# Sample attentions: values of the first four sequences weighed between the key chunks of the other four, loads queued in that order, three key banks

## The reference, cut to what matters

```python
# B: dilated windows over a cache of 2048 keys, 4 heads x 64, 8 sequences
logit = einsum('nthe,ntjhe->nthj', q, kg) + bias        # per dilation group (128,1), (512,4), (2048,16)
out   = merge_by_denominators(stats)                    # softmax over the union, multiplicities by the groups
# C: sparse attention over 4096 cached keys, 256 of them selected per query by an indexer
logit = einsum('nqhe,nqkhe->nqhk', q, kg) + bias        # only selected keys
out   = einsum('nqhk,nqkhe->nqhe', softmax(logit), vg)
```

## Time and profile before

| what | us |
|---|---|
| timed runs, median of 3 | 3127.01 (3124.59 to 3127.49) |
| profiled execution | 3129.59 |
| its span | 3127.8 |
| stage B (1449.2 to 1589.7) | 140.5 |
| stage C (1589.7 to 1834.8) | 245.1 |
| mlp (1834.8 to the end) | 1293.0 |

### The profile page before, as it was taken

The page is one execution under the profiler, slowest core; times in us unless marked ns, Lnnn a source line. Parts: engine busy times, 40 slices in busy tenths (PEclk is TensorE's granted clock), DMA queues, the critical chain, the costliest instruction groups (busy, mean ns, idle before and its releaser), DMA issues. The chain is left out here.

```text
span 3127.8 us, 33968 instructions
## 1 busy us (share of the span) xinstructions
PE 2659.0 (85%) x13588; PEld 1692.1 (54%) x13604; DVE 1136.5 (36%) x2070; ACT 666.8 (21%) x1346; POOL 366.8 (12%) x352
## 2 busy tenths in 40 slices
PE   7999995085788987886638769999999999999998
PEld 3444442032667776454425434566666666888843
DVE  0007999655666665484615202100000000000033
ACT  1122221032334544574303200100000000000011
POOL 1000000101444431000016520000000000000000
PEclk9999997576799999798768879999999999999999
DMA  6111110241335532414779772301101113110010
GB/s 238 51 42 51 41 41 20 100 114 39 112 97 161 150 126 77 155 38 131 254 216 359 284 269 101 115 27 40 40 27 40 40 28 105 39 38 29 11 34 33
DMA packets 170291, 305.86 MB, mean 98 GB/s; under 512 B 48536, under 2 KB 121448, under 8 KB 167866
## 3 DMA queue, kind: packets, MB, share of 16 engines
q1 hardware_dynamic: 145154, 175.87, 18.0%
q0 software_dynamic: 23136, 93.01, 8.2%
q10 hardware_dynamic: 1864, 35.08, 3.3%
HBM read 262.76 MB, written 68.29 MB: 106 GB/s over the span
## 5 line engine op out<-in xcount | busy, mean ns | idle before, releaser
L929 PE MATMUL m_B<-m_big,m_wdB 128*128 128x363 f32 (+1 forms) x2112 | 646.1, 468 | 3.2 <-issue 3.2
L929 PEld LDWEIGHTS m_B<-m_big,m_wdB 128*128 128x128 f32 x2112 | 400.4, 190 | 248.0 <-issue 5.0
L384 PE MATMUL i_psM<-i_w,i_xnT 128*128 128x477 f32 x1024 | 418.3, 567 | 2.3 <-ACT i_xnT L232 2.3
L384 PEld LDWEIGHTS i_psM<-i_w,i_xnT 128*128 128x128 f32 x1024 | 192.8, 191 | 213.5 <-issue 206.5
L791 DVE TENSOR_TENSOR m_actT<-m_wdB,m_B 128x363 f32 (+3 forms) x66 | 35.1, 532 | 604.1 <-PE m_B L929 604.1
L683 ACT ACTIVATE m_wdB<-m_B 128x363 f32<-128x363 f32 (+1 forms) x66 | 31.2, 473 | 599.0 <-PE m_B L929 599.0
L971 PE MATMUL m_B<-m_wdA,m_actT 128*128 128x256 f32 x704 | 152.4, 379 | 0.8 <-DVE m_actT L791 0.8
L971 PE MATMUL m_B<-m_wdB,m_actT 128*128 128x256 f32 x704 | 152.6, 379 | 0.0
L971 PEld LDWEIGHTS m_B<-m_wdA,m_actT 128*128 128x128 f32 x704 | 133.7, 190 | 19.5 <-DVE m_actT L791 1.4
L971 PEld LDWEIGHTS m_B<-m_wdB,m_actT 128*128 128x128 f32 x704 | 133.5, 190 | 18.8 <-issue 0.8
L649 POOL TENSOR_TENSOR m_rstd<-m_ms,m_half 128x1 f32<-128x1 f32 x18 | 9.9, 553 | 1133.3 <-DVE m_ms L759 1133.3
(11 more groups left out here) (414 smaller groups left out, 3587.0 us busy)
## 6 DMA issues: line engine op xcount, KB each, us to landing
b_Kp<-b_k SPq DMA_DIRECT2D x32, 512.0 KB, 10.5
b_Vp<-b_v SPq DMA_DIRECT2D x32, 512.0 KB, 11.2
o_bk<-b_k ACTq DMA_DIRECT2D x8, 2040.0 KB
o_bv<-b_v ACTq DMA_DIRECT2D x8, 2040.0 KB
i_w<-w_in POOLq DMA_DIRECT2D x8, 1908.0 KB, 29.9
proj<-i_stage SPq DMA_DIRECT2D x64, 238.5 KB, 2.0
m_wdB<-w_gate SPq DMA_DIRECT2D x22, 512.0 KB, 4.0
m_wdB<-w_up SPq DMA_DIRECT2D x22, 512.0 KB, 5.2
```

The lines of the kernel that those rows point to most:

```text
L384: mm = nc.tensor.matmul(psM[:, c % 2, 0:CHW], xnT[:, t % 2, k, :], w[:, k, c * CHW:(c + 1) * CHW], start=(k == 0), stop=(k == KO - 1))
L929: mm = nc.tensor.matmul(B[:, bank, 0:r1 - r0], wgu[:, i, u, k, :], hnT[:, k, r0:r1], start=(k == 0), stop=(k == KO - 1))
```

## The change

Transposed probabilities get a bank of their own (4) while keys are still transposed, and keys keep three (0, 1, 3). For the chunks behind the key loop, probabilities use all four. The first NCH - 1 chunks of the first group (MIXED: 3 in B, 7 in C) are transposed, copied and weighed inside the key loop, one in each step from chunk NCH + 1 on (LAG = 1): `turn_keys(ch+1)`, `turn_probs(k)`, `products(ch)`, `weigh(k)` with k = ch - NCH - 1. ACT's order follows: the copy of probabilities k stands behind the copies of the next chunk's keys, and the exponential of the second group behind the last copy of the first group. The load queue takes values between key chunks in the order in which they are wanted. DVE's order is unchanged but for the bank number.

```diff
...
     TOT = KEYS + DEC
     COL = COL_C if sparse else COL_B
     KS, VS = 8, 12
-    TURN_BANKS = (0, 1, 3, 4)
+    TURN_BANKS, PROB_BANK = (0, 1, 3), 4
+    LAG = 1
+    MIXED = NCH - LAG
+    prob_bank = lambda k: PROB_BANK if k < MIXED else (0, 1, 3, 4)[(k - MIXED) % 4]
     LOGIT_BANKS = (2, 7)
     with ExitStack() as ctx:
         sb = lambda n, s, dt=F32: ctx.enter_context(nc.sbuf_tensor(f"{tag}_" + n, s, dt))
...
                             eng.wait_ge(S["pv"], (k - VS) // 4 + 1)
                         piece_dma(eng, "c_v" if sparse else "b_v", k, Vp[:, k % VS, :], V_in[k % VS])
 
-                keys(range(2 * CH))
-                values(range(VS))
-                keys(range(2 * CH, 4 * CH))
-                values(range(VS, 4 * CH))
+                chunk = lambda ch: range(4 * ch, 4 * ch + 4)
+                ready = VS // 4
+                for ch in range(NCH):
+                    keys(chunk(ch))
+                    if ch >= NCH - ready:
+                        values(chunk(ch - NCH + ready))
+                for ch in range(NCH, CH):
+                    keys(chunk(ch))
+                    if ch - 2 >= NCH + LAG:
+                        values(chunk(ch - 2 - NCH - LAG + ready))
+                for ch in range(max(MIXED - 2, 0) + ready, CH):
+                    values(chunk(ch))
 
             @block.sync
             def _(sp):
...
                     act.wait_ge(S["keysT"], b + 1)
                     if ch >= 2:
                         act.wait_ge(S["products"], ch - 1)
-                    nc.scalar.activation(KpT[:, ch % 2, n, i, :], B[:, TURN_BANKS[b % 4], :], ACT.Copy)\
+                    nc.scalar.activation(KpT[:, ch % 2, n, i, :], B[:, TURN_BANKS[b % 3], :], ACT.Copy)\
                         .then_inc(keysT_out[i], 1)
 
                 def softmax(g):
...
                     nc.scalar.activation(logit[:, g, :], logit[:, g, :], ACT.Exp, bias=nmx[:, g:g + 1],
                                          accum_out=den[:, g:g + 1]).then_inc(S["prob"], 1)
 
+                def evac_probs(k):
+                    act.wait_ge(S["probT"], k + 1)
+                    if k >= 2:
+                        act.wait_ge(S["pv"], k - 1)
+                    nc.scalar.activation(PT[:, k % 2, :, :],
+                                         B[:, prob_bank(k), :].rearrange("p (j q) -> p j q", j=4),
+                                         ACT.Copy).then_inc(S["PT"], 1)
+
                 for ch in range(CH):
                     for n in range(4):
                         for i in range(1 if sparse else 2):
                             evac_keys(4 * ch + n, i)
-                    if ch == NCH + 1:
+                    if ch == NCH + LAG:
                         softmax(0)
+                    if ch > NCH + LAG:
+                        evac_probs(ch - 1 - NCH - LAG)
+                for k in range(MIXED - 1, NCH):
+                    evac_probs(k)
                 softmax(1)
-                for k in range(CH):
-                    act.wait_ge(S["probT"], k + 1)
-                    if k >= 2:
-                        act.wait_ge(S["pv"], k - 1)
-                    nc.scalar.activation(PT[:, k % 2, :, :],
-                                         B[:, TURN_BANKS[k % 4], :].rearrange("p (j q) -> p j q", j=4),
-                                         ACT.Copy).then_inc(S["PT"], 1)
+                for k in range(NCH, CH):
+                    evac_probs(k)
 
             @block.vector
             def _(dve):
...
                     dve.wait_ge(S["keysT"], b + 1)
                     if ch >= 2:
                         dve.wait_ge(S["products"], ch - 1)
-                    nc.vector.tensor_copy(KpT[:, ch % 2, n, i, :], B[:, TURN_BANKS[b % 4], :])\
+                    nc.vector.tensor_copy(KpT[:, ch % 2, n, i, :], B[:, TURN_BANKS[b % 3], :])\
                         .then_inc(keysT_out[i], 1)
 
                 def logits(g, c):
...
                         pe.wait_ge(K_in[k % KS], 16 * (k // KS + 1))
                         for i in range(2):
                             b = 2 * k + i
-                            if k >= 2:
-                                pe.wait_ge(keysT_out[i], k - 1)
+                            if b >= 3:
+                                pe.wait_ge(keysT_out[(b - 3) % 2], (b - 3) // 2 + 1)
                             for j in range(4):
-                                mm = tp(B[:, TURN_BANKS[b % 4], P * j:P * j + P],
+                                mm = tp(B[:, TURN_BANKS[b % 3], P * j:P * j + P],
                                         Kp[:, k % KS, B_W * j + P * i:B_W * j + P * i + P], ident[:, :])
                             mm.then_inc(S["keysT"], 1)
 
...
                 if sparse:
                     pe.wait_ge(spread_at, 1)
                     pe.wait_ge(unsel_in, 32)
-                for ch in range(CH):
-                    if ch + 1 < CH:
-                        turn_keys(ch + 1)
-                    products(ch)
-                    if ch % NCH == NCH - 1:
-                        new_products(ch // NCH)
 
                 def turn_probs(k):
                     g, c = k // NCH, k % NCH
-                    if k >= 4:
-                        pe.wait_ge(S["PT"], k - 3)
+                    before = max(k - 3, MIXED if k - MIXED >= 3 else 0) if k >= MIXED else k
+                    if before:
+                        pe.wait_ge(S["PT"], before)
                     if c == 0:
                         pe.wait_ge(S["prob"], g + 1)
                     for j in range(4):
-                        mm = tp(B[:, TURN_BANKS[k % 4], P * j:P * j + P], logit[:, g, 512 * c + P * j:512 * c + P * j + P],
+                        mm = tp(B[:, prob_bank(k), P * j:P * j + P], logit[:, g, 512 * c + P * j:512 * c + P * j + P],
                                 ident[:, :])
                     mm.then_inc(S["probT"], 1)
 
-                turn_probs(0)
-                for k in range(CH):
+                def weigh(k):
                     g, c = k // NCH, k % NCH
-                    if k + 1 < CH:
-                        turn_probs(k + 1)
                     if c == 0:
                         if g:
                             pe.wait_ge(S["out"], 1)
...
                         mm.then_inc(S["out_new"], 1)
                         pe.wait_ge(S["on"], g + 1)
                         mm_(B[0:32, 5, 0:B_W], pick[:, :], on[:, :]).then_inc(S["picked"], 1)
+
+                for ch in range(CH):
+                    k = ch - NCH - LAG
+                    if ch + 1 < CH:
+                        turn_keys(ch + 1)
+                    if k >= 0:
+                        turn_probs(k)
+                    products(ch)
+                    if ch % NCH == NCH - 1:
+                        new_products(ch // NCH)
+                    if k >= 0:
+                        weigh(k)
+                turn_probs(MIXED)
+                for k in range(MIXED, CH):
+                    if k + 1 < CH and k + 1 != NCH:
+                        turn_probs(k + 1)
+                    weigh(k)
+                    if k + 1 == NCH:
+                        turn_probs(NCH)
 
 
 def phase_index_c(nc, D, mix_):
```

## The result

Median of 5 runs 3110.22 us (3104.80 to 3112.99) against 3127.01 (3124.59 to 3129.27, 5 runs of the kernel before on the same chip): ratio 0.9944, 95% interval 0.9930 to 0.9958. Forecast 3107, range 3094 to 3120. The profiled execution took 3110.22, its span 3108.4; it is the median run, where the one of the kernel before lay 2.6 us above its median, so the spans differ by 19.4 us and the medians by 16.8. Of all runs told of here one, of c_only (3193.46 us), was disturbed, and its ratio is taken without it.

A forecast was written before the change was run, and what follows sets the result against it. Each sample-attention stage was taken as its bytes over 410 GB/s plus stretches in which nothing is loaded, which the change fills. Gains of 14 us in b and 6 in c, off the 3127.01 median, gave 3107, range 3094 to 3120.

The forecast's parts named there:

- b 1: Start of stage b: values queued before key 8 may add up to 5.1 us to bias rows and keys; taken at 0.
- b 2 and 3: Stage b, weighings in and behind the key loop: 7.8 us added beside 6.78 us of TensorE idling; taken at 0.
- b 4: End of stage b: last values meet the mask's stores (4.1 us); last weighing starts at 1566.6, not 1581.15; gain 14 us.
- c 1 and 2: Stage c to step 9's end, 1716: early chunks barely change, three key banks cost 0.2 us a step, 1.5 at softmax(0).
- c 3: Stage c's mixed steps 10 to 14: keys queued behind values awaiting weighings; 11.1 us a step, step 14 ending at +54.3.
- c 4: Stage c after step 14: issuing values 32 onwards sets the end, 1820.5, which is 8.6 us earlier.
- c 5: TensorE's clock in stage c's mixed steps: assumed granted at 0.87, which leaves c a gain of 6 us.
- A: Rival, c's mixed loop: longer landings delay keys behind waiting values; c +38, total +24 us, 3151; 5%.
- B: Rival, mixed steps run at a cold clock: c loses 5 us, b gains 12; 3120; 10%.
- C: Rival, nothing gained at b's start and mask stores cost in full: b gains 7 to 9, c 5; 3114; 10%.
- D: Rival, transfers overlap better than counted: b gains 23 us, c 11; 3093; 13%.
- E: Rival, weighings wait, so slots come free as late as now; only bank cost left, +3 to +7; 3132; 2%.

The follow-up runs named there:

- c_only: The change made in stage c alone, stage b left as the old function, against the kernel before: 3119.98 us, ratio 0.9972.
- b_block: The changed kernel, but stage b's first 12 value pieces are queued in one block behind the first group's keys, as before the change: 3102.23 us.
- unsel_rows: The changed kernel, but stage b stores the selection mask in whole rows of 4 KB, so c masks other keys: 3104.09 us.
- keys_first: The changed kernel, but in c's mixed loop the next keys are queued ahead of the values that wait for a weighing: 3096.85 us.

## Why the prediction was right, and where it was not

The median lies 3 us above the forecast, inside the range. By the stages, however, two misses of opposite sign stand in the sum: b was to give 14 and gave 10.7 (mean of four 9.5), c was to give 6 and gave 9.7 (mean of five 10.9).

- **The bound** (each stage waits for its last values; transfers stand still in between): right. Nothing but standing time went away, 4 GB/s became 206, and the mlp stayed at 1293.
- **b 1, the start, taken at 0: wrong, and it is the step that failed in b.** The prediction named the cause, up to 5.1 us of values ahead of the bias rows, and then let it go. "Before K19 there are 32 pieces either way" is true and not to the point: it counts pieces ahead of one key, while the bias rows come by another queue and share the engines with whatever is in flight, 12 pieces in place of 8. And the 5.23 us gap could not hide it, because it waited for keys that became late by as much. DVE began 3.0 later, greatest(1) came 2.9 later. b_block took the cause away and got DVE's start back.
- **b 2 and 3, the weighings beside the key loop: right.** The wait before new_products(1) fell from 6.78 to 0.62, and softmax(1) was held only by the late maximum.
- **b 4, values 20 to 31 behind the stores: right mechanism, priced too low.** The last weighing was to start 117.4 us after the stage's start and started at 121.2; weigh(2), which frees the slots, ended 2.7 late, and from there it took 24.6 in place of 23.5 (26.7 to 27.0 in the three other kernels with the same b, so this profile was the luckiest). The stores, charged with 4.1, cost 4.2 by the stages of unsel_rows; where the block is also restored they cost 6.5. The stores had runs of 128 B, and runs of 4 KB gave this time back. By the Trainium skill, DMA: Bandwidth & Descriptors, Specifications, a transfer needs pieces of at least 512 B to run at line rate. The runs agree with that: 215 GB/s against 414 with the engines as busy.
- **c 1 and 2, T(9): right.** Forecast 126.3 us after the stage's start, measured 126.3 (1706.69, the end of weigh(0)). The banks' 0.2 a step was 0.23, the stall at softmax(0) 0.87 where 1.5 was counted.
- **c 3, the mixed loop: right.** Five steps were to last 54.3 and lasted 53.0 (to 1759.74), with the waits for keys in the queue's order, as keys_first shows. The single steps, 8.1, 13.5, 9.7, 11.3 and 10.5 us, were not all within the 10 to 12 that were named as a sign.
- **c 4, the tail: right.** From T(14) to the end of the last weighing 50.2 forecast, 51.1 measured. Without the clock the gain was to be 8.6; the end of the last weighing came 8.8 earlier in the stage (230.5 against 239.3). Behind it the stage ended another 0.9 us sooner (4.9 against 5.8), which the prediction did not have.
- **c 5, the clock, 0.87 and -2.6: wrong, and it is the step that failed in c.** The granted clock was 0.97 over 1706.7 to 1759.7, the full 2.4 GHz nearly throughout, at 82% busy, and in keys_first 1.00; over half of TensorE's time in a mixed step is transposes. By the Trainium skill, TensorE: Matmul & The Clock Gate, Part 4: PE-mode transpose, the full clock does not engage for transposes. By that rule it would have been 0.50; the trace disagrees with it.

Of the rivals, A (latency) did not come about: no step exceeded 14 us (the longest was 13.5). The landings that it was held against, 7.8 us or less, went up to 8.3 in the earlier trace rows, which changes nothing. B is refuted by 0.97. C (start of b not hidden, b 7 to 9, c 5) had b's mechanism right, and c's gain wrong. D did not come, since the stores held the engines (215 GB/s at a share of 1.06). E is refuted by the weighings at 1704.76 and after. Beside the single steps, three of the signs named were missed: the last weighing of b outside 1565 to 1569 (1570.4 by the old kernel's times), the clock above 0.8 to 0.9, and c shorter than 237 (235.4). The range was wide enough for the two misses by their sizes, and it was luck that they cancelled: 20.4 us in the two stages for the 20 of the sum, with -3.3 in b and +3.7 in c (-4.5 and +4.9 by the means). That the median still fell by 3 less is in the 1.3 us of the stages ahead of b and in the profiled run of the kernel before, which lay 2.6 above its median, while the one after is the median itself.

## What to carry to other kernels

When loads are reordered, count what is in flight beside every other queue's transfers, not only the pieces ahead of one load; a load that waits for nothing is sent at once and takes bandwidth from one that is wanted sooner. In a queue that holds all behind a wait, put the load whose slot is free ahead of the one that waits: here that alone was worth 13 us, beside the 17 to 18 of the whole change before it. A small store beside a full load stream is priced by its run length: half a megabyte in runs of 128 B cost some 4 to 6.5 us, and the layout could be mended for nothing where it is read.

## What the runs showed of the hardware

- The granted clock did not follow the busy share alone: 0.80 at 66% busy before (1764 to 1826) and 0.88 at 63% after (1765 to 1807). Both stretches are weighings that wait for values. One difference is that the second comes behind mixed steps at 0.97; whether it is the cause no run tests.
- One core took 379 GB/s over 42 us beside its weighings and 376 over keys_first's mixed steps, with TensorE 96% busy in the latter.
- Two stores of 0.25 MB each in runs of 128 B, beside a full stream of loads, brought the DMA engines to 215 GB/s over 5 us at a share of 1.06; with runs of 4 KB it was 414 at 1.02.
- The length of a stage repeated within 1 us where it was as before, and within 2.6 (b) and 2.4 (c) as changed and 3.6 (b with the block: 126.3 to 129.9), where weighings, keys and values share the queue.
